# The first sixteen K blocks of the down projection by seven quadrant products, and weight forms split in five instructions

## The reference

```python
z  = rmsnorm(x) @ w_in            # 1024 -> 7 * 1024
# u, v, B, C, h, gate_A, gate_B: spatial gating, short convolution, two merges
x  = x + m @ w_o
x  = x + (silu(xn @ w_gate) * (xn @ w_up)) @ w_down   # xn = rmsnorm(x); 1024 -> 2816 -> 1024
y  = rmsnorm(x)
```

## Time and profile before

| | |
|---|---|
| median of 3 runs | 860.22 us (860.22 to 860.46) |
| the profiled execution, span | 859.0 us |
| PE busy | 849.9 us, 99% |
| DVE busy | 657.9 us, 77% |
| ACT busy | 420.7 us, 49% |

### The profile page before, as it was taken

How to read it: one execution, slowest core, us unless ns; L and a number is a source line. 1 busy time by engine, 2 the same in 40 slices (tenths; PEclk the granted TensorE clock), 3 DMA queues, 4 the chain that set the end, 5 groups by cost and what they waited for, 6 DMA issues and landing times.

```text
span 859.0 us, 17035 instructions
## 1 busy us (share of the span) xinstructions
PE 849.9 (99%) x6740; PEld 848.0 (99%) x6740; DVE 657.9 (77%) x1112; ACT 420.7 (49%) x761; POOL 18.6 (2%) x23
## 2 busy tenths in 40 slices
PE   9999999999999999999999999999999999999996
PEld 9999999999999999999999999999999999999996
DVE  6868878789999999844578899997634699995343
ACT  7432225556666666642165776665221366664121
POOL 0000000000000000000000000000000000000230
PEclk9999999999999999999999999999999999999998
DMA  8333315132323232331551233222322222223312
GB/s 300 113 100 101 105 51 157 46 131 84 125 85 117 89 109 97 102 100 50 176 174 50 66 116 112 99 98 74 110 74 91 93 98 99 98 79 116 92 31 105
DMA packets 54841, 88.28 MB, mean 103 GB/s; under 512 B 2176, under 2 KB 45184, under 8 KB 49408
## 3 DMA queue, kind: packets, MB, share of 16 engines
q1 hardware_dynamic: 54784, 87.49, 30.8%
HBM read 85.10 MB, written 2.38 MB: 102 GB/s over the span
## 4 chain that ended last, share of the span: by engine, by line
PE 95%; DVE 3%; ACT 1%; issue 1%; POOL 0%; DVEq 0%; POOLq 0%
PE ps_main L593 13%; PE ps_main L591 13%; PE ps_main L592 13%; PE ps_main L795 13%; PE ps_main L796 13%; PE ps_main L797 13%; PE ps_t L796 4%; PE ps_t L795 4%; PE ps_t L797 4%; DVE w_lo L1632 1%; PE ps_g L734 1%; PE ps_g L636 1%; PE ps_t L618 1%; PE ps_main L648 0%; PE ps_main L647 0%
## 5 line engine op out<-in xcount | busy, mean ns | idle before, releaser
L591 PE MATMUL ps_main<-act_hi,w_hi 128*128 128x272 f32 x940 | 272.3, 290 | 0.0
L593 PE MATMUL ps_main<-act_hi,w_lo 128*128 128x272 f32 x940 | 271.8, 289 | 0.0
L592 PE MATMUL ps_main<-act_lo,w_hi 128*128 128x272 f32 x940 | 270.4, 288 | 0.0
L795 PE MATMUL ps_main<-xf_hi,w_hi 128*128 128x272 f32 x924 | 267.1, 289 | 0.1
L796 PE MATMUL ps_main<-xf_lo,w_hi 128*128 128x272 f32 x924 | 267.1, 289 | 0.0
L797 PE MATMUL ps_main<-xf_hi,w_lo 128*128 128x272 f32 x924 | 266.9, 289 | 0.0
L591 PEld LDWEIGHTS ps_main<-act_hi,w_hi 128*128 128x128 f32 x940 | 177.0, 188 | 0.2
L592 PEld LDWEIGHTS ps_main<-act_lo,w_hi 128*128 128x128 f32 x940 | 177.1, 188 | 0.0
L593 PEld LDWEIGHTS ps_main<-act_hi,w_lo 128*128 128x128 f32 x940 | 176.7, 188 | 0.0
L795 PEld LDWEIGHTS ps_main<-xf_hi,w_hi 128*128 128x128 f32 x924 | 174.0, 188 | 0.3 <-ACT parts L1065 0.3
L797 PEld LDWEIGHTS ps_main<-xf_hi,w_lo 128*128 128x128 f32 x924 | 173.9, 188 | 0.0
(11 more groups left out here) (247 smaller groups left out, 980.1 us busy)
## 6 DMA issues: line engine op xcount, KB each, us to landing
w_raw<-in_w_quads_dram SPq DMA_DIRECT2D x20, 1024.0 KB, 4.8
w_raw<-in_w_gate_dram SPq DMA_DIRECT2D x11, 1024.0 KB, 4.8
w_raw<-in_w_up_dram SPq DMA_DIRECT2D x11, 1024.0 KB, 4.8
w_raw<-in_w_in_dram SPq DMA_DIRECT2D x6, 1024.0 KB, 5.1
w_raw<-in_w_down_dram SPq DMA_DIRECT2D x8, 768.0 KB, 4.8
w_raw<-in_w_down_dram SPq DMA_DIRECT2D x8, 640.0 KB, 4.5
w_raw<-in_w_pa_dram SPq DMA_DIRECT2D x4, 1024.0 KB, 5.6
w_raw<-in_w_pb_dram SPq DMA_DIRECT2D x4, 1024.0 KB, 5.4
```

The lines of the kernel that those rows point to most:

```text
L591: pe.matmul(out, whi, xhi, start=(opens and k == order[0]), stop=False)
L592: pe.matmul(out, whi, xlo, start=False, stop=False)
L593: last = pe.matmul(out, wlo, xhi, start=False, stop=(closes and k == order[-1]))
L795: pe.matmul(out, whi, xhi, start=opens and k == 0, stop=False, skip_group_check=not opens)
```

## The change

- The feed forward part becomes one list of 30 units, `FFN`: four gate/up pairs and four down units, twice, then three gate/up pairs; written out, where loops stood before. Sixteen of the 22 hidden blocks go through down units of seven products (two output blocks each, from the weights `w_down_quads`, laid out on the host), the last six through `down` as before (8 units of 36 matmuls).
- The hidden blocks of the first two parts are needed as seven forms too: VectorE makes four sums of their quadrants in three instructions and the low parts in five, ScalarE the high parts in five.
- `first_down` runs the first down unit of a part in another order, so that the last hidden blocks are asked for later.
- The down units drain into the residual directly (`down`), which is first multiplied by the root of the mean square: `newton = msq * rstd`, spread over the partitions by `spread` a second time (behind product 2 of unit 4), in place of the reciprocal.
- In all 50 quadrant units the seven weight forms are cast and split in five groups, `GROUPS`: product 0, products 1 and 2, product 4, products 3 and 5, product 6. `FORM_AT` says which group a product waits for.
- `rest_of_sums` follows K block 0 of the second part of the last block.

```diff
-A11, A12, A22, S1, S2, S3, S4 = range(7)
+A11, A12, A22, S3, S2, S1, S4 = range(7)
+GROUPS = {0: slice(0, 1), 2: slice(1, 3), 4: slice(4, 5), 5: slice(3, 6, 2), 6: slice(6, 7)}
+FORM_AT = (1, 2, 2, 4, 3, 4, 5)
+PAIRS = (4, 4, 3)
+FFN = tuple((kind, c, n) for c, pairs in enumerate(PAIRS)
+            for kind, n in [(kind, n) for n in range(pairs) for kind in ("gate", "up")] + [("down", n) for n in range(4 if c < 2 else 0)])
...
         # tensor
+            def first_down(q, s, c):
+                made = 5 * (KQ * c + KQ - 1)
+                def there(x, k):
+                    if k == KQ - 1:
+                        pe.wait_ge(hf_ready, made + {A12: 1, A22: 1, A11: 2, S3: 3, S1: 3, S2: 4, S4: 5}[x])
...
+                for f, blocks in ((0, range(KQ - 1)), (1, range(KQ - 1)), (5, range(KQ - 2))):
+                    pe.wait_ge(form_lo, NGROUP * q + FORM_AT[f])
+                    part(f, blocks)
+                part(0, (KQ - 1,))
+                part(1, (KQ - 1,))
+                part(5, (KQ - 2,))
+                for n, f in enumerate((2, 3, 4)):
+                    pe.wait_ge(part_copied, 4 * q + 1 + n)
+                    part(f, range(KQ))
+                part(5, (KQ - 1,))
+                pe.wait_ge(part_copied, 4 * q + 4)
+                pe.wait_ge(form_lo, NGROUP * q + NGROUP)
+                part(6, range(KQ))
...
-            last_block(0, {0: lambda: turn_y(3, 0), 7: rest_of_sums})
-            last_block(1, {3: lambda: turn_last(0), 4: lambda: last_sums(0)})
+            last_block(0, {0: lambda: turn_y(3, 0)})
+            last_block(1, {0: rest_of_sums, 3: lambda: turn_last(0), 4: lambda: last_sums(0)})
...
         # scalar
             def first_forms(p, q, j, s):
...
-                for f in range(4):
-                    form(q, 0, f)
+                form(q, 0, 0)
+                form(q, 0, 2)
...
             form(QG, 0, 4)
+            form(QG, 0, 5)
             second_square(KD - 1)
             copy_part(QG, 0, 2)
-            form(QG, 0, 5)
             form(QG, 0, 6)
...
+                made = {0: lambda: h_second(pair - 1, m - 1), 1: lambda: h_first(pair - 1, m - 1),
+                        3: lambda: h_sums(pair - 1, m - 1), 4: lambda: h_sum2(pair - 1, m - 1),
+                        6: lambda: h_sum4(pair - 1, m - 1)}
+                if n == 2:
+                    made[5] = root_diagonals
...
         # vector
+            def gate(n):
...
                 form(q, 0, 6)
+                if n:
+                    last_of(n)
+                next_sums(n, 0)
+                if split:
+                    h_first_sums(pair)
+                next_form(n, 0)
+                if split:
+                    low_second(pair)
...
+                next_sums(n, 1)
+                if split:
+                    h_sum2(pair)
+                if split:
+                    low_first(pair)
+                next_sums(n, 2)
+                if split:
+                    h_sum4(pair)
...
+                next_form(n, 2)
                 second_sums(q, 0, gate_sb)
+                if split:
+                    low_sums(pair)
                 second_rest(q, 0, gate_sb)
...
+                next_form(n, 4)
+                if split:
+                    low_sum2(pair)
                 first_sums(q, 0, gate_sb)
+                if split:
+                    low_sum4(pair)
+                next_form(n, 5)
...
+            def down(n):
...
+                if m == 0:
+                    low_second(pair)
+                    last_of(n)
+                    h_first_sums(pair)
+                    h_sum2(pair)
+                    low_first(pair)
+                    low_sums(pair)
+                    h_sum4(pair)
+                    low_sum2(pair)
+                    form(q, s, 6)
+                    low_sum4(pair)
+                else:
+                    form(q, s, 6)
+                    last_of(n)
...
```

More of the change, by code:

```diff
@@ L768, in _, with xn_forms, x_forms, h_forms @@
                 unit(p, j, s, A0)
-            def seven(q, s, first=None, behind={}, bank_c=None, a_free=0, forms=(xf2_hi, xf2_lo)):
-                for f, (_, _, x, bank) in enumerate(PRODUCTS):
-                    if f == 0 and not (isinstance(q, int) and q < 2):
+            def xn_forms(x, k):
+                return xf_hi[:, x, k, :], xf_lo[:, x, k, :]
+            def x_forms(x, k):
+                return xf2_hi[:, x, k, :], xf2_lo[:, x, k, :]
+            def h_forms(x, k):
+                return (s4_hi[k][:], s4_lo[k][:]) if x == S4 else (hf_hi[:, x, k, :], hf_lo[:, x, k, :])
+            def product(q, s, f, blocks, forms, there=None):
+                _, _, x, bank = PRODUCTS[f]
+                out, opens = banks[s][bank], f in (0, 1, 5)
+                for k in blocks:
+                    if there is not None:
+                        there(x, k)
+                    whi, wlo = f_hi[:, f, k * P:(k + 1) * P], f_lo[:, f, k * P:(k + 1) * P]
+                    xhi, xlo = forms(x, k)
+                    pe.matmul(out, whi, xhi, start=opens and k == 0, stop=False, skip_group_check=not opens)
+                    pe.matmul(out, whi, xlo, start=False, stop=False, skip_group_check=not opens)
+                    last = pe.matmul(out, wlo, xhi, start=False, stop=k == KQ - 1, skip_group_check=not opens)
+                if blocks[-1] == KQ - 1:
+                    last.then_inc(form_used, 1)
+            def seven(q, s, first=None, behind={}, bank_c=None, a_free=0, forms=x_forms):
+                def there(x, k):
+                    pe.wait_ge(xf_ready, NPROD * (first + k) + X_ORDER.index(x) + 1)
+                for f in range(NPROD):
+                    if f == 0 and q >= 2:
                         pe.wait_ge(quad_out, 4 * q - 4)
@@ L786, in seven, with there, part @@
                         pe.wait_ge(part_copied, 4 * q + 4)
[L787 to L798, removed]
+                    pe.wait_ge(form_lo, NGROUP * q + FORM_AT[f])
+                    product(q, s, f, range(KQ), forms, there if first is not None else None)
                     if f in behind:
                         behind[f]()
+            def first_down(q, s, c):
+                made = 5 * (KQ * c + KQ - 1)
+                def there(x, k):
+                    if k == KQ - 1:
+                        pe.wait_ge(hf_ready, made + {A12: 1, A22: 1, A11: 2, S3: 3, S1: 3, S2: 4, S4: 5}[x])
+                def part(f, blocks):
+                    product(q, s, f, blocks, h_forms, there)
+                pe.wait_ge(quad_out, 4 * q - 4)
+                pe.wait_ge(hf_ready, made)
+                for f, blocks in ((0, range(KQ - 1)), (1, range(KQ - 1)), (5, range(KQ - 2))):
+                    pe.wait_ge(form_lo, NGROUP * q + FORM_AT[f])
+                    part(f, blocks)
[9 more added lines that the diff above has]
+                part(6, range(KQ))
             p = ph["quads"]
```

511 lines of the change are left out of this document (302 added, 209 removed).

## The result

The changed kernel takes **869.75 us** (median of 4 runs, 869.45 to 870.21), the kernel before 860.34 us beside it: ratio 1.0108, 95% interval 1.0096 to 1.012. Slower, by 9.4 us, and 1.75 us beyond the predicted range. Of the 9.4 us, 8.5 lie in the span (867.5 against 859.0).

A forecast was written before the change was run, and what follows sets the result against it. TensorE, busy 99%, was taken to bound the kernel, with VectorE right behind in gate/up. Terms -12.1 + 1.3 + 8.2 + 3.0 + 1.0 + 1.2 = +2.6 on 859.0 gave 861.6, 862.8 us as a run; range 855 to 868.

The forecast's parts named there:

- Matmuls removed, -12.1: Down projection: 960 matmuls in place of 1056, 96 fewer at 126.1 ns, all on the chain, -12.1 us.
- Spread, +1.3: Behind product 2 of unit 4: five fp32 matmuls made once more, +1.3 us.
- A pair costs VectorE 22.1: Gate/up pairs of the first two parts: VectorE needs 22.1 us, 0.9 more than TensorE takes.
- Rival B: Merging saves 0.16 in place of 0.09, a pair costs 21.6, 860.3 us, no change; chance 0.17.
- Lag of the parts, +8.2: First two parts: VectorE's lag reaches TensorE, 3.4 us in the first and 4.8 in the second, +8.2 us.
- More is paid either there or at the first down unit, and in sum it is the same: Lag beyond about 0.5 us free is paid at up units' product 6 or the first down unit, same sum.
- Entry, +3.0: First gate unit: product 3 waits for its form, merged with product 5's; TensorE stands from 480.56 to 483.6, +3.0 us.
- Last stage, +1.0: Last down stage: with six K blocks, the last hidden blocks are needed at K block 4, before they are done, +1.0 us.
- Tail, +1.2: Last block: the first part's norm has one K block beside it, not five; +1.2 us, between 0 and 2.5.
- rival C: Three TensorE stalls of about 3 us halve the clock afterwards, three times 1.5 us, 867 to 868 us; chance 0.14.
- Rival A: VectorE keeps up, so the lag term is 0 to 1; 854.6 to 855.6 us as a run, faster; chance 0.22.

The follow-up runs named there:

- the single forms: The changed kernel with seven single weight forms in place of the five groups in all units, down projection still by seven products: 861.89 us, ratio 1.0015.
- the added instruction: The 860.28 us kernel with one more 128x272 VectorE instruction in each of six gate units (a low half made twice): 864.1 us, ratio 1.0044.
- the version with single forms: Best version: changed kernel with seven single forms, the last block's first half taken earlier, last unit's scalings ahead of product 6's form in gate units: 860.28 us, ratio 0.9997.
- the grouped version with gaps of 1.9 us (862.48): Changed kernel with product 3's early form, gate's first half scaled during a cast, first down unit's quadrant scaled and cast earlier, last block reordered: 862.48 us, ratio 1.0022.
- the same version without the tail's order: Changed kernel with product 3's early form, gate's first half scaled during a cast, first down unit's quadrant earlier, last block not reordered: 863.41 us, ratio 1.0033.

## Why the prediction was wrong

Slower was the likeliest outcome by the forecast and it came, but not by this much: 862.8 forecast, 869.75 measured, 1.75 outside the range. By its own steps:

1. **Matmuls removed, -12.1.** Right: the gaps and the rest close to within 0.1 us with it.
2. **Spread, +1.3.** Right.
3. **A pair costs VectorE 22.1.** 22.2. The merged form stepped 1.13 to 1.14 as said, and the wait for the merged cast was 0.39 to 0.47. Rival B, by which grouping pays more and a pair costs 21.6, is excluded by that, and the single forms show what grouping is worth: 22.30 against 22.20, 0.1 us a pair.
4. **Lag of the parts, +8.2.** 8.9. The second part came out as said (4.6 for 4.8), the first was taken too low (4.3 for 3.4). "More is paid either there or at the first down unit, and in sum it is the same" held in three experiments that tried to break it. What it missed is that the split decides about the clock.
5. **Entry, +3.0.** 3.1; product 3 began at 483.65 for a forecast 483.6.
6. **Last stage, +1.0.** 1.04.
7. **Tail, +1.2.** 1.6, within its 0 to 2.5. Behind the first part's norm VectorE came to the second part at 858.55, 1.4 us after the last matmul of it had ended, and TensorE stood for 1.9 us.

These come to +3.8 on the span, 1.2 above the forecast's +2.6, and the sum by them alone would have been inside the range. **The step that failed is the one that left the clock out of the sum**: the forecast held full speed through three gaps of 2 to 3 us, and put "the stalls cost the clock" aside as rival C with a chance of 0.14. In its place the runs showed a granted clock of 0.51 behind each of the three gaps, 4.3 us in all and 0.5 more in the tail; filling the gaps took every one of these stretches away. The prediction had named this sign of its being wrong itself, a granted clock below 1.00 ahead of the tail. C's mechanism was right in place and size (1.5, 1.4 and 1.4 us for three times 1.5); its 867 to 868 fell short by what the terms above were too small (1.2 us), by 0.3 on the clock, and by the time around the span: the profiled execution took 869.45 us around a span of 867.5, 1.95 us where I had added 1.2. That 1.2 compared a span and a run time of different executions; the kernel before has 1.7 us around its span in every run beside the experiments (860.62 against 858.9, for one), and all versions with the new down units have 1.85 to 2.0. C was priced low because the trace of before has no such gap and so could show nothing; that was no evidence against it.

Rival A (VectorE keeps up) is excluded by the windows of the changed kernel, and for the version with single forms by the added instruction.

Beyond the prediction: why 96 matmuls less bring nothing even at best. In the version with single forms 12.1 us are saved; 1.3 are spent on the spread, 8.5 on the waits in the two parts, 1.0 before the last stage and 0.8 in the tail. The span is 0.5 us shorter than before (858.5 against 859.0), and 0.2 more around it hides part of that. No experiment removed VectorE work without paying for it elsewhere, so whether a lighter pair would bring the gain is open; the added instruction shows the slope only upwards.

## What to carry to other kernels

When a matmul engine at 99% is relieved, look at the second engine stage by stage: here it was busy for 19.7 of 21.2 us in the stage that got its new work. Once it is the slower one, moving waits about mostly moves the gap; whether less work on it would help more was not tested here.

A gap on TensorE is not priced by its length alone. The one of 3.2 us cost 4.7; lag that was paid in pieces of about 1 us cost what it measured. Where a lag can't be removed, pay it in small pieces or fill it. And merging two instructions can put work ahead of its due time: ask of each half when it is awaited.

## What the runs showed of the hardware

- Gaps here are counted from start to start, less 0.126 us, one profiled execution of each kernel. After a TensorE gap of 3.2 us the next 13 to 16 matmuls of 272 columns started every 0.227 us (granted clock 0.51, the 1.2 GHz level) in 2 of 2 profiled cases. After gaps of 2.0 to 2.4 us they did so in 7 of 11, after 1.5 to 1.95 us in 4 of 10 (three of them with a further gap of 0.6 us just behind), after 1.45 us or less never. The same gap of 2.06 us in one trace did both. The tail's gap is left out of this count. Such kernels also scatter more: the best version's 11 runs lie within 0.7 us, the 11 of the grouped version with gaps of 1.9 us (862.48) within 2.2. Of the same version without the tail's order, the profiled execution had no slow stretch ahead of the tail (862.11 us, clock 0.997), while the other four took 862.93 to 864.22 us at 0.993 to 0.995: one profile doesn't show what the clock does in every run.
- At 0.51 of the clock a matmul with its weight load stepped 0.227 us against 0.126, 1.8 times and not 2.
- GpSimd's 128x272 subtraction took 0.77 to 1.13 us and lengthened VectorE's instructions beside it by 0.47 and 0.58 us; a busy VectorE steps on by 0.35 us with the same work.
